# The scale and shift of norm 1 made as columns and put on behind the transposes, and the first projection groups grown slice by slice

## The reference, cut to what matters

```python
ada = silu(c) @ w_ada + b_ada                       # (1, 6*1024)
shift1, scale1, gate1, shift2, scale2, gate2 = jnp.split(ada, 6, axis=-1)
h = rms_norm(x, norm1_g) * (1 + scale1) + shift1
proj = h @ w_in                                     # (512, 2304): qa ka va qb kb vb
o_a = windowed_gqa(qa, ka, va, sink, t5_table)      # 8 heads, 2 of keys
o_b = neighbourhood_attention(qb, kb, vb, rpb)      # 8 heads
x = x + gate1 * (norms(o_a, o_b) @ w_out)
h2 = rms_norm(x, norm2_g) * (1 + scale2) + shift2
x = x + gate2 * peer(h2)      # each token: 8 heads x 16 experts, rows gathered from memory
```

## Time and profile before

| | us |
|---|---|
| runs (3) | 2245.67, 2247.22, 2257.49; median 2247.22 |
| profiled execution, first to last instruction | 2244.4 |
| PE, DVE, ACT, POOL busy | 2010.7, 1356.7, 858.5, 930.4 |
| mean granted TensorE clock, share of full | 0.984 |
| DMA packets of the gather queue | 536.90 MB, 58.1% of 16 engines |

### The profile page before, as it was taken

One profiled execution on the slowest core, in us unless ns is written; L12 is line 12 of the kernel. 1 busy time (PEld: TensorE's weight loads), 2 busy tenths in 40 slices (PEclk: granted clock), 3 DMA queues, 4 the chain that ended last, 5 costly groups with the idle time before them and its releaser, 6 DMA issues. The chain is left out here.

```text
span 2244.4 us, 21634 instructions
## 1 busy us (share of the span) xinstructions
PE 2010.7 (90%) x6736; PEld 1105.7 (49%) x6736; DVE 1356.7 (60%) x3074; ACT 858.5 (38%) x2260; POOL 930.4 (41%) x633
## 2 busy tenths in 40 slices
PE   7999898898898899988767889898889999999999
PEld 5787543333333333333323333333335566888887
DVE  6333456787778777787666667857445563433432
ACT  2453323454444444444333334434334343321321
POOL 0793025576656666665445656555630010000000
PEclk9999999999999999999899999999999999999999
DMA  9443339999999999999999999999972003233221
GB/s 378 178 149 124 121 125 413 421 419 417 417 411 416 416 417 412 416 418 407 418 416 405 419 421 408 418 412 414 417 301 110 1 1 94 94 101 105 95 94 57
DMA packets 120292, 655.12 MB, mean 292 GB/s; under 512 B 11097, under 2 KB 29553, under 8 KB 49393
## 3 DMA queue, kind: packets, MB, share of 16 engines
q0 software_dynamic: 73728, 536.90, 58.1%
q1 hardware_dynamic: 43504, 111.51, 13.8%
q10 hardware_dynamic: 2944, 5.33, 0.6%
HBM read 651.60 MB, written 2.10 MB: 291 GB/s over the span
## 5 line engine op out<-in xcount | busy, mean ns | idle before, releaser
L980 PE MATMUL bank<-ring,diag 128*128 128x512 f32 x1912 | 936.6, 617 | 184.5 <-ACT diag L1509 182.1
L641 POOL DMA_INDIRECT ring<-in_uv,idx x508 | 780.8, 1537 | 535.6 <-PE bank L980 232.0
L2143 DVE CUSTOM_DVE_ANT_0 zjunk<-ring,h 128x1024 bf16<-128x1024 f32 x508 | 622.3, 1225 | 368.2 <-DMA ring<-in_uv,idx 365.8
L980 PEld LDWEIGHTS bank<-ring,diag 128*128 128x128 f32 x1912 | 342.3, 191 | 718.4 <-ACT diag L1509 453.0
L1500 ACT ACTIVATE zg<-z 128x1 f32<-128x1 f32 x512 | 103.5, 202 | 726.6 <-DVE z L2143 726.3
L1509 ACT ACTIVATE diag<-ident,weight 128x128 f32<-128x128 f32 x482 | 193.4, 401 | 15.7
L2313 DVE TENSOR_TENSOR ml_lo<-mlp_raw,ml_hi 128x2048 fp32r<-128x2048 f32 x32 | 73.4, 2293 | 114.5 <-ACT ml_hi L1633 114.5
L896 PE MATMUL bank<-w_q,h2T 128*128 128x512 f32 x256 | 130.7, 602 | 3.5 <-ACT h2T L1406 1.8
L577 POOL TENSOR_SCALAR stats<-stats 128x1 f32<-128x1 f32 (+2 forms) x25 | 8.0, 319 | 292.5 <-ACT slot L1591 109.0
L1633 ACT ACTIVATE ml_hi<-mlp_raw 128x2048 fp32r<-128x2048 f32 x32 | 61.1, 1908 | 121.8 <-PE bank L679 107.6
L677 PE MATMUL bank<-hTm_hi,ml_hi 128*128 128x512 f32 (+2 forms) x272 | 103.6, 381 | 1.6 <-DVE hTm_lo L2308 1.6
(11 more groups left out here) (252 smaller groups left out, 2694.0 us busy)
## 6 DMA issues: line engine op xcount, KB each, us to landing
ada_w<-in_w_ada SPq DMA_DIRECT2D x24, 1024.0 KB
mlp_raw<-in_w_up SPq DMA_DIRECT2D x16, 1024.0 KB, 5.5
mlp_raw<-in_w_down SPq DMA_DIRECT2D x16, 1024.0 KB, 5.0
win_raw<-in_w_in SPq DMA_DIRECT2D x9, 1024.0 KB, 6.8
w_q<-in_w_query SPq DMA_DIRECT2D x8, 1024.0 KB, 10.1
ring<-in_uv,idx POOLq DMA_INDIRECT x508
w_kvb<-in_w_in SPq DMA_DIRECT2D x8, 640.0 KB, 36.3
x<-in_x SPq DMA_DIRECT2D x8, 512.0 KB, 13.0
```

The costliest lines, as they stand in the source:

```text
L641: e.indirect_dma_start(row(n), None, a["uv"], bass.IndirectOffsetOnAxis(ap=idx[i][:, j:j + 1], axis=0)).then_inc(s[f"d_ring{n % RING}"], 16)
L980: t = e.matmul(bank[2 * (i % 2) + half], diag[added_by_pe(n) % 4], row(n)[:, 1024 + 512 * half:1536 + 512 * half], start=(j == 0), stop=(j ...
L2143: e.tensor_tensor_reduce(out=zjunk, in0=row(n)[:, 0:1024], in1=h2[:, i, :], scale=1.0, scalar=0.0, op0=ALU.mult, op1=ALU.add, accum_out=z[ ...
```

## The change

The load order is turned round: x comes first, then ada chunks and w_in chunks mixed (0, 4, w_in 0, 1, 5, w_in 1, 2, 6, 3, 7, w_in 2), and chunk 7 in two halves. Each tile of x is multiplied by its root in place, transposed by PE as it is, and copied to `xT`. Shift and scale of norm 1 are made as columns: PE writes chunk n as two columns of PSUM, either straight from the weights (`col_direct`, chunks 4, 1, 2: 16 matmuls with one moving column) or from a sum (`col_total`: DVE sums chunks 0, 5, 6, 3 and half of 7; POOL the other half). DVE adds bias and gain to a pair of chunks (`columns`), and ACT applies scale and shift to a slice of `xT` (`whole`), and makes the high part (`high`); DVE makes the low part (`low`). Items 0 to 3 grow two slices at a time as these come, in four banks. Gate chunks 8 and 10 go to POOL, 9 and 11 to DVE. POOL also makes win_low(1). `ADA_ACT` gains chunks 10, 18 and 21, and `ADA_STEP` and `MULTIPLY_AT` move the totals and the products of chunks 10 to 23 to later steps. `PIECES`, the steps in which the items begin, and the order of POOL's list from chunk 12 on stay as they are.

```diff
-ADA_PE = (1, 3, 5, 7, 8, 9, 10)
-ADA_ACT = (12, 13, 14, 16, 19, 22)
-ADA_STEP = {14: 0, 15: 2, 16: 5, 17: 8, 18: 11, 19: 14, 20: 17, 21: 21, 22: 23, 23: 27}
-MULTIPLY_AT = {u + half: (n, half) for n, u in ((16, 1), (19, 10), (22, 18)) for half in (0, 1)}
+COL_ORDER = (4, 0, 1, 5, 2, 6, 3, 7)
+COL_PE = (4, 1, 2)
+ADA_DVE = {0: 8, 5: 16, 6: 24, 3: 32, 7: 36, 9: 45, 11: 54}
+ADA_POOL = (7, 8, 10, *range(12, 24))
+ADA_ACT = (10, 12, 13, 14, 16, 18, 19, 21, 22)
+ADA_STEP = {10: 0, 11: 1, 12: 3, 13: 4, 14: 6, 15: 9, 16: 12, 17: 14, 18: 17, 19: 20, 20: 23, 21: 25, 22: 28, 23: 31}
+MULTIPLY_AT = {u + half: (n, half) for n, u in ((14, 3), (16, 6), (18, 11), (19, 14), (21, 18), (22, 21)) for half in (0, 1)}
...
 def item_bank(n):
-    return 6 + n % 2 if n < 6 else 6
+    return (6, 7, 4, 5, 6, 7)[n] if n < 6 else 6
...
 def low_done(c):
-    return ("v_wlo", c + 1) if c < 4 else ("g_wlo", c - 3)
+    return ("g_wlo", 1 if c == 1 else c - 2) if c == 1 or c > 3 else ("v_wlo", max(c, 1))
...
+            e.dma_start(cols1, a["cols1"]).then_inc(s["d_c"], 16)
             for i in range(NT):
                 load_x(i)
+            load_ada(0)
+            load_ada(4)
+            load_win(0)
+            load_ada(1)
+            load_ada(5)
+            load_win(1)
+            load_ada(2)
+            load_ada(6)
+            load_ada(3)
+            load_ada(7)
+            load_win(2)
+            q.wait_ge(s["p_col"], col_done(4))
+            q.wait_ge(s["v_ada"], ada_summed(5))
+            e.dma_start(bias_a, a["bias_a"].rearrange("h p j -> p h j")).then_inc(s["d_ba"], 16)
             load_ada(8)
             load_ada(9)
...
+            for i in range(NT):
+                q.wait_ge(s["a_ss1"], i + 1)
+                inverse_root(f"first{i}", ss1[:, i:i + 1], 1.0 / D, EPS)
+            win_low(1)
+            half_columns()
+            ada_columns(8)
+            ada_columns(10)
             ada_columns(12)
             ada_columns(13)
...
+            def col_direct(n):
+                q.wait_ge(s["v_c"], 3)
+                q.wait_ge(s[f"d_ada{n}"], ada_loaded(n))
+                if n < 4 and n >= 2:
+                    q.wait_ge(s["v_col"], 3 * (n - 1))
+                for half in (0, 1):
                     for k in range(8):
+                        t = e.matmul(col_of(n, half), ada_w[n][:, k, 128 * half:128 * half + 128], c_tmp[:, k:k + 1], start=(k == 0), stop=(k == 7))
+                t.then_inc(s["p_col"], 1)
...
+            col_direct(4)
+            col_total(0)
+            col_direct(1)
+            both(0, (0, 1))
+            col_total(5)
+            col_direct(2)
+            both(0, (2, 3))
+            both(2, (0, 1))
+            col_total(6)
+            both(2, (2, 3))
+            both(0, (4, 5))
+            col_total(3)
+            col_total(7)
+            both(2, (4, 5))
+            both(0, (6, 7))
+            both(2, (6, 7))
+            item(4, range(8))
+            ada_total(8)
+            ada_total(9)
+            item(5, range(4))
+            scores(0)
+            scores(1)
+            item(5, range(4, 8))
...
+            def whole(k):
+                part = xT[:, k, :]
+                q.wait_ge(s["v_col"], 3 * (k // 2 + 1))
+                q.wait_ge(s["a_xT"], 10)
+                e.activation(part, part, ACT.Identity, bias=shift_col[:, k:k + 1], scale=scale_col[:, k:k + 1]).then_inc(s["a_full"], 1)
+
+            def high(k):
+                q.wait_ge(s["a_full"], k + 1)
+                e.activation(hT[0][:, k, :], xT[:, k, :], ACT.Copy).then_inc(s["a_hT"], 1)
...
+            split_win(0)
+            for m in range(4):
+                for k in (2 * m, 2 * m + 1):
+                    whole(k)
+                    high(k)
+                if m == 0:
+                    split_win(1)
+
...
+            copy_item(0)
+            copy_item(1)
+            split_win(2)
+            copy_item(2)
+            copy_item(3)
+            split_win(3)
+            ada_products(10, range(8))
+            shift_chunk(8)
+            shift_chunk(9)
+            ada_products(12, range(8))
+            ada_products(13, range(8))
...
+            def columns(m):
+                b, shift, scale = bank[m % 2], slice(2 * m, 2 * m + 2), slice(8 + 2 * m, 10 + 2 * m)
+                q.wait_ge(s["p_col"], max(col_done(m), col_done(m + 4)))
+                e.tensor_tensor(shift_col[:, shift], b[:, shift], cols1[:, shift], ALU.add).then_inc(s["v_col"], 1)
...
+            def low(k):
+                q.wait_ge(s["a_hT"], k + 1)
+                e.tensor_tensor(hT[1][:, k, :], xT[:, k, :], hT[0][:, k, :].bitcast(F32), ALU.subtract).then_inc(s["v_hT"], 1)
...
+            for i in range(NT):
+                scaled_x(i)
+            ada_columns(0, range(8))
             win_low(0)
+            columns(0)
+            low(0)
+            low(1)
+            ada_columns(5, range(8))
+            columns(1)
+            low(2)
+            low(3)
+            ada_columns(6, range(8))
+            columns(2)
+            ada_columns(3, range(4))
+            low(4)
+            low(5)
+            ada_columns(3, range(4, 8))
+            ada_columns(7, range(4, 8))
+            columns(3)
+            low(6)
+            low(7)
+            ada_columns(9, range(8))
             win_low(2)
+            win_low(3)
...
             copy_item(4)
-            win_low(3)
+            ada_columns(11, range(8))
             copy_item(5)
```

More of the change, by code:

```diff
@@ L69, in ada_place, with ada_loaded, summed_by, col_done @@
 def ada_place(n):
-    return n % 8 if n < 12 else 8 + n % 2
+    return n if n < 10 else n - 10 if n < 12 else 8 + n % 2
 def ada_bank(n):
-    return n % 2 if n < 14 else 7
-def ada_use(n):
-    return n // 8 + 1 if n < 12 else (n - 12) // 2 + 3
-def ada_summed(n):
-    return 9 * (n // 2 + 1) if n < 8 else 45 if n < 12 else sum(4 if m in ADA_ACT else 5 for m in range(12, n + 1))
+    return n % 2 if n < 10 or n in (11, 13) else 7
+def ada_loaded(n):
+    if n < 8:
+        return 16
+    return 32 if n < 10 else 48 if n < 12 else 32 * ((n - 12) // 2 + 2)
+def ada_summed(n):
+    if n in ADA_DVE:
+        return ADA_DVE[n]
+    return 3 + sum(4 if m in ADA_ACT else 5 for m in ADA_POOL[1:ADA_POOL.index(n) + 1])
+def summed_by(n):
+    return "v_ada" if n in (9, 11) else "g_ada"
+def col_done(n):
+    return COL_ORDER.index(n) + 1
 def item_chunk(n):
@@ new lines, in col_total @@
+            def col_total(n):
+                q.wait_ge(s["v_ada"], ada_summed(n))
+                if n == 7:
+                    q.wait_ge(s["g_ada"], 3)
+                for half in (0, 1):
+                    cols = slice(128 * half, 128 * half + 128)
+                    if n == 7:
+                        e.matmul(col_of(n, half), ada_pool[n][:, cols], one[:, 0:1], start=True, stop=False)
+                    t = e.matmul(col_of(n, half), ada_sum[n][:, cols], one[:, 0:1], start=n != 7, stop=True)
+                t.then_inc(s["p_col"], 1)
@@ L759, in items, with both @@
                         yield
-            q.wait_ge(s["v_hT"], 10)
-            for n in range(6):
-                if n == 5:
-                    scores(0)
-                    scores(1)
-                item(n, range(8))
-                if n == 1:
-                    ada_total(11)
-                if n in (3, 4):
-                    ada_total(n + 9)
+            def both(n, ks):
+                item(n, ks)
+                item(n + 1, ks)
+            col_direct(4)
[21 more added lines that the diff above has]
+            item(5, range(4, 8))
             def transposes(u):
@@ L776, in transposes @@
                     q.wait_ge(s["v_va"], 1)
+                    q.wait_ge(s["a_copy"], 8)
                 elif u % 2:
@@ L1737, in _ @@
-            for n in range(9):
-                if n < 8 and n not in ADA_PE:
-                    ada_columns(n)
-                if n >= 5:
-                    scale_chunk(n - 1)
-            def norm1(i):
-                q.wait_ge(s["g_root"], rooted("first"))
-                q.wait_ge(s["v_scale"], 4)
-                q.wait_ge(s[f"d_x{i}"], 16)
-                q.wait_ge(s["p_hT"], 2 * (i - 1))
-                e.scalar_tensor_tensor(hn[i % 2], x[:, i, :], ss1[:, i:i + 1], slot[0], ALU.mult, ALU.mult).then_inc(s["v_hn"], 1)
-                q.wait_ge(s["v_hn"], 2 * i + 1)
-                q.wait_ge(s["a_shift"], 4)
-                e.tensor_tensor(hn[i % 2], hn[i % 2], slot[1], ALU.add).then_inc(s["v_hn"], 1)
```

288 lines of the change are left out of this document (130 added, 158 removed).

## The result

The changed kernel takes **2276.9 us** (median of 5 runs, 2275.69 to 2289.03) against 2247.22 for the kernel before (5 runs beside it, 2245.67 to 2257.49): ratio 1.0132, 95% interval 1.0109 to 1.0155. It is slower, as forecast, and 7.7 us slower than the forecast's 2269.2.

The account below looks back on a forecast made before the run. In the attention steps PE is the bound, with POOL right behind it. 27.4 us lost in the steps less 5.4 won in the head is 22.0 slower: 2247.2 + 22.0 = 2269.2 us, range 2238 to 2282.

Parts of the forecast that it names:

- the stated forecast: Whole kernel: S between 84 and 92, 19 to 28 us slower, 2266 to 2275; chance 0.50.
- the slices don't pay: Rival, head: items gain nothing, S at 94 or more, 29 us slower or above, 2276 to 2284; chance 0.13.
- S: End of DVE's copies of item 5, which opens the attention steps: 92.89 before, 87.5 forecast.
- Item 10: Step 4: PE waits for POOL's win_low(4) behind chunks 14 and 15; start at S+34.0, +11.9 us.
- Item 14: Step 12: waits for win_low(5) behind chunk 18; 31.0 us after item 10 against 22.55, +8.5 us.
- Item 16: Step 15: waits for win_low(6) behind chunks 19 and 20; 27.2 us after item 14 against 21.85, +5.3 us.
- The loads of the chunks hide under this chain: Steps: chunk n's load is asked for when n-2 is summed, with a POOL chunk or low half between.
- of which I let 12.4 fall on DVE's chain: Head: of 17.4 us of POOL's work beside DVE, 12.4 lengthen DVE's chain and 5 fall into its waits.
- below, their price is bounded by nothing, as DVE's chain hides them: Head: PE's 16 one-column matmuls take at most 4.2 us, beside DVE's work.
- DVE and POOL hardly meet: Rival, head: S near 75, head gains 18, steps take back 27, 9 us slower, 2256; chance 0.17.
- Faster: Rival, steps: items don't wait for POOL; S at 75 minus a stall of 4, 14 us faster, 2233; chance 0.12.
- nothing behind the steps took the shift up: Rival, behind the steps: a wait for the DMA of biases or w_out absorbs the shift, 2247; chance 0.08.

Follow-up runs that it names:

- e1: The changed kernel with POOL's low halves of w_in chunks 4 and 6 moved ahead by two ada chunks, that of 5 by one: 2259.7 us.
- e6: e1 with ACT's products of chunks 16, 21 and 22 one step later and win_low(7) ahead of chunk 22: 2256.7 us.
- e9: e6 with ACT's products of chunk 14 one step earlier, in steps 2 and 3: median 2255.7 us.
- e10: e9 with four of DVE's eight sums of chunk 11 moved ahead of its copy of k: 2250.8 us, ratio 1.0017.
- e12: The kernel before the change, with POOL's low half of w_in chunk 4 moved back behind the sums of chunk 18: 2265.2 us.
- e5: The changed kernel with the low half of w_in chunk 1 made by DVE and not by POOL: median 2281.5 us, lowest run 2272.4.
- e4: The changed kernel with only POOL's low half of w_in chunk 4 moved, ahead of chunk 14: lowest run 8.0 us lower than the changed kernel's.
- e8: The changed kernel with 16 added 128-column identity products between the one-column matmuls of chunks 4 and 1: S at 89.62 against 89.58.
- e2: The changed kernel with POOL starting chunk 8 only when DVE has summed chunk 7: lowest run 2277.0 us.

## Why the prediction was right, and what it missed

The mechanism and the three waits came as forecast. The time, 2276.9, lies in the whole range (2238 to 2282), but above the 2266 to 2275 given for the stated forecast, and in the band of the rival "the slices don't pay", whose sign (S at 94 or more) did not come. Two of its sums are slightly off: the middle of 85.9 and 89.7 is 87.8, not 87.5, and S from 84 to 92 with 27.4 lost gives 18.5 to 26.5 slower, not 19 to 28.

**The steps: right.** All three waits came where they were forecast, released by what was forecast, and 12, 6 to 7 and 3 to 4 us were 12.01, 5.68 and 3.25. Term by term, from the starts in PE's timeline:
- Item 10: S+34.0 forecast, 125.31−89.58 = S+35.7 measured, so +13.7 (35.73 less 22.06 before) for +11.9. POOL took up chunk 14 at 106.52, S+16.9 for S+15.1; that is the 1.8. The other rows fit: 14, 15 and the low half took 18.7 us (106.52 to 125.25) for 18.9.
- Item 14: 30.4 behind item 10 for 31.0, +7.85 for +8.5. Item 16: 27.2 for 27.2, +5.4 for +5.3.
- From item 16 to the gather: 161.8 against 159.7 before, +2.1 for the +1.7 put down to the clock.

The sum is 29.0 lost in the steps for 27.4, and less 3.3 that is the 25.65 us at the gather. The three waits have 20.9 of the 29.0. The clock has most of the other 8.1: its shares of full were 0.76 (88 to 94 us), 0.63 (125 to 130), 0.56 (155 to 160) and 0.83 (180 to 190), where they were 1.00 before, some 7 us as an estimate. That these waits are POOL's list and not the head is shown twice: e1, e6, e9 and e10 took them away with the head's order unchanged but for chunk 11, and e12 made one in the kernel before, whose head it left alone. Why POOL comes so late has two reasons that no run parts: chunks 8 and 10 were added, and ACT's products come in later steps. In this execution POOL was done with chunk 13 at 95.61 and stood 10.91 us for the products of 14, so at item 10 it was the second that held.

"The loads of the chunks hide under this chain" was right only while the chain was that long: ACT stood 6.01 us at the load of chunk 16, and with POOL's list mended (e1) PE paid 5.73 of it.

**The head: S nearly right, by two errors that cancel, and by luck.** Forecast 87.5, measured 89.58, and the last slice at 65.5 as forecast. But the step "of which I let 12.4 fall on DVE's chain" was too high: before the last slice DVE's rows are longer by 4.27 (chunk 5), 1.02 and 1.22 (two column products), 0.45 (a low slice) and 1.61 (chunk 3), 8.6 us in sum. What filled the difference is "below, their price is bounded by nothing, as DVE's chain hides them". Each chunk's 16 one-column matmuls stand as one line of 32 records in PE's timeline:

```profile
16.45 4.12 PE L757 MATMUL bank<-c_tmp,ada_w 128*128 128x1 f32 x32
...
21.29 6.96 PE L757 MATMUL bank<-c_tmp,ada_w 128*128 128x1 f32 x32
```

They took 6.96 us at the low clock (0.50), 4.12 where the clock fell on the way (0.88), and 3.70 in e5 at 1.00. At 49.89 DVE waited 5.40 us for a total that stood behind the columns of chunk 2 and eight slices of items in PE's list, most of them at the low clock. Hidden in the first two pairs, not in the third. Behind the last slice PE began the last matmul of item 5 at 87.04, and chunk 11 held its copy until 88.85; splitting the chunk (e10) moved S by 1.65 us. The luck is here: the forecast allowed up to 4 us for chunk 11, and in e4, with the same head, its meeting with POOL put S at 92.84, outside the bounds of 73.5 to 92.

**What no step had.** 25.65 us at the gather became 30.2 at its end: the gather took 1333.2 us against 1328.7. In the twelve kernels of the experiments, with the same work, it took 1327.8 (e12) to 1332.1 (e8), so the 4.5 us are about the spread between executions, and no experiment looked for their cause. Of the 7.7 by which the forecast fell short, the head has 2.1 and the steps 1.6; the other 4.0 are of that size.

**The rivals.** "DVE and POOL hardly meet" fell to the 7.88. "Faster" named its own test, item 10 less than 26 us after S; it was 35.7. The slices paid at most a little (S of 89.6 after and 92.84 in e4, not 94; 92.89 before), and nothing behind the steps took the shift up.

The Trainium skill, page SBUF — State Buffer, section Who interferes with whom, says that a DVE instruction with two SBUF inputs contends with a GpSimd instruction that reads SBUF. The traces agree, and for scalar_tensor_tensor too: 7.88 against 3.61 with the kernel otherwise alike (e5).

## What to carry to other kernels

When a change puts work at the front of a serial list on an engine that is not the bound, ask for each product further down how long before its first use it was ready: here the low half had 9.5 us and came 19.8 us later (its end at 125.25 for 105.45), and its consumer is the engine that bounds the kernel. Then look at who is next: with POOL's list mended, the same stage hung on ACT's products and on the loads that wait for POOL's sums, and only four edits together (e10) brought the 25 us at the gather back, to a tie. Where two engines are busy in one stretch, moving the work of one ended one meeting and made another (e2, e5), so both lists have to be followed to the end of the stretch, not to the end of the wait that was mended.

## What the runs showed that was not expected

- Work of POOL that meets DVE holds even a very small instruction with two inputs in SBUF for the full rest of POOL's: the product of a 128x2 column takes 0.16 us alone, and 1.18, 1.38 (after) and 2.29 (e2) under POOL. The sum just ahead of it, one of whose inputs is in PSUM (L1827), took its 0.16 us at 49.89 although POOL's instruction ran from 49.12 to 51.51.
- An engine that is sooner can end a stretch later. With PE's clock full from 74 to 78 us, item 4 was ready about 1 us sooner, DVE's chunk 11 met POOL's chunk 10 in another place, and S was some 3 us later (e4 against after, the same head).
- TensorE's granted clock was at its lower level (0.50, 1.2 GHz) from 20 to 28 us though its records leave no idle time there. Ahead of that stood 16 one-column matmuls, and with wide ones between them (e8) the fall came some 2 us later. What sets it stays open.
- A low half that fills a wait costs little where it stands: taken out ahead of chunk 16 in e12, 4.56 us of work brought 16's sums forward by only 2.1 us (105.39 to 103.27).
